# VectorE's low parts and the differential norm, moved from ahead of the next row maximum to behind it

## The chip, the core and the metric

The kernel runs on one core of one Trainium2 chip. The metric is the time of one execution on the device in microseconds (us); lower is better. The kernel before took 1900.06 us (median of three runs, 1899.64 to 1900.58).

## What is computed

A trunk of two layers on x of 512 x 1024 (float32). Each layer is a feed-forward block, a mixer and a second feed-forward block, each followed by a layer norm. The change touches the mixer alone:

```python
proj = x @ w_in
# FoX heads: 6 of width 64
s = einsum(q, k) * scale + (c_q - c_k);  p = softmax(causal(s));  y = p @ v
# differential heads: 4, each with two maps of width 32
p = softmax(causal(einsum(q, k) * scale - slope * dist))
a = p[0] - lam * p[1];  o = a @ v
o = o * rsqrt(mean(o * o) + eps) * norm_g * (1 - lam_init)
# SGU heads: 6
y_sgu = u * (tril(w_s) @ layer_norm(g) + b_s)
out = concatenate([y_fox, y_diff, y_sgu]) @ w_out
```

## The kernel before

Every large product is made of three matmuls: each float32 operand is split into a high part (ScalarE rounds it into an fp32r tile) and a low part (VectorE or GpSimd subtracts the high part from the original), and TensorE adds high x high, high x low and low x high. A low part is thus a subtraction that has to wait for ScalarE's copy. The whole program is written out by hand as one instruction list for each engine, with semaphores between them. No scheduler reorders anything: each engine takes its list in order, and a wait in it holds all that stands behind.

**The attention stage.** Per layer there are 5 bodies b = 0 to 4. A body is a pair of heads. Bodies 0, 2 and 4 are FoX, bodies 1 and 3 (`DIFF_AT`) are differential. A body has 8 steps k = 0 to 7: two heads times four blocks of 128 queries. The text numbers the 40 steps of a layer G = 8b + k. The block t = G mod 4 has (t+1)*128 keys, so steps get longer from t = 0 to t = 3.

In step G TensorE (`heads`, from L1276) issues, in this order: the scores of step G (L1291, and the mask L1293), three matmuls of other work, the value products of step G-2 (L1313), the transposes of the probabilities of step G-1 (L1303), three more matmuls of other work. The other work is a generator: in bodies 0 to 2 the projection of the queries and keys of body b+2 (`project`, L1216; queries in the body's steps k = 0 to 3, keys in k = 4 to 7), in bodies 3 and 4 the output projection with the head chunks that are ready (`early_output`, L1011). In four steps, (b,k) = (0,1), (0,5), (2,1) and (2,5), so G = 1, 5, 17 and 21, four transposes of a chunk of the output (`turn_y`, L1242) close the step. They write into bank 7 or bank 6, the same PSUM banks that the projections use, and so wait for `qk_ok`, the count of query and key low parts done:

```python
pe.wait_ge(qk_ok, (l * BODIES + at[0] + 1) * 2 + (3 if at[1] > NT else 2))   # L1228
```

For G = 1 and G = 17 that is the key low part of body 1 and of body 3, for G = 5 and G = 21 the query low part of body 2 and of body 4: each is the part that VectorE does in that step's neighbourhood.

ScalarE in step G: `exp` of step G (L919, one for each map; it waits for the row maximum), `p_out` of step G-1 (L926, the copy of the transposed probabilities that the value products read), then at k = 0 the high part of the keys of body b+1 (L858) and half of a weight tile (`key_half`, L713), at k = 4 the high part of the queries of body b+2 (L851) and `query_half` (L713 too) of the weights of body b+3, and in the step after a `turn_y` its high part (`y_hi`, L932).

VectorE in step G: `row_max` (L1898, one for each map), `inverse` (L1905, a reciprocal, FoX only), `output` of step G-2 (L1930, which waits for that step's value products), `early_add` (L1540, bodies 3 and 4), in differential bodies `mix` (L1913, L1915, L1919: reciprocals, weight, and the sum of the two maps, which waits for both exponentials), and then the pieces that the change moves:

- `key(b+1)` at k = 0 (L1811): low part of the keys
- `query(b+2)` at k = 4 (L1806): low part of the queries
- `y_lo` (L1859): low part of an output chunk, in the step after its transposes, and in body 4 at k = 1, 2 and 7
- `rms` (L1874, L1878, L1885, L1890): the four stages of the differential norm, in bodies 2 and 4. GpSimd makes the reciprocal root between the second and the third (`norm_root`, L597 and L599)

SyncE (`put_query`, `put_key`, L462) then writes the query and key parts of a body to DRAM in 12 transfers each, and behind `put_key(b)` it loads the weights of body b+2 into the tile `rawA` (`fill`, L395), which `query_half` on ScalarE waits for. GpSimd loads the stacked queries and keys of a body back from DRAM (`load_stack`, L652) before its scores.

Of the kernel before, what the change touches and what calls it, by code (L numbers as in the profile page):

```python
# [48 lines left out]
BODIES = FOX_P + DIFF_P  # L49
# [12 lines left out]
STEPS = 2 * NT  # L62
# [13 lines left out]
ALL = BODIES * STEPS  # L76
# [45 lines left out]
def build(nc, x_in, a_w, b_w, d_w, gb_row, gb_col, mix_row, mix_col, ws_in, lamv, out):  # L122
    ctx = ExitStack()
    with ctx:
# [244 lines left out]
        def is_diff(G):  # L369
            return G // STEPS in DIFF_AT  # L370
# [1093 lines left out]
        def _(dve):  # L1464
# [329 lines left out]
            for l in range(L):  # L1794
# [98 lines left out]
                def row_max(G):  # L1893
                    w_ = (G % NT + 1) * P
                    for m in range(2 if is_diff(G) else 1):
                        i = 2 * (G % 2) + m
                        dve.wait_ge(s_done[m], count(l, G, m))
                        v.tensor_reduce(negm[:, i:i + 1], bank[i][:, 0:w_], AX.X, ALU.max,  # L1898
                                        negate=True).then_inc(max_ok[m], 1)
# [32 lines left out]
                query(1)  # L1932
                dve.wait_ge(nlam1_ok, l + 1)
                wait_here(5)
                for G in range(ALL):
                    b, k = divmod(G, STEPS)
                    row_max(G)
                    last_key = k == 0 and b == EARLY_BODY
                    if last_key:
                        key(b + 1)  # L1940
                    if G and not is_diff(G - 1):
                        inverse(G - 1)
                    if G >= 2:
                        output(G - 2)
                    if G - EARLY_BODY * STEPS in ADD_STEP:
                        early_add(ADD_STEP[G - EARLY_BODY * STEPS])
                    if is_diff(G):
                        mix(G)
                    if k == 0 and b + 1 < BODIES and not last_key:
                        key(b + 1)  # L1950
                    if k == NT and b < EARLY_BODY:
                        query(b + 2)
                    if (b, k - 1) in TURNS:
                        y_lo(TURN_AT.index((b, k - 1)))
                    if b == BODIES - 1 and k in LATE_TURNS:
                        y_lo(LATE_TURNS[k])
                    if b in RMS_AT and k in RMS_AT[b]:
                        rms(DIFF_AT.index(b - 1), RMS_AT[b].index(k))
                inverse(ALL - 1)
                output(ALL - 2)  # L1960
                early_add(6)
                early_add(7)
                output(ALL - 1)
# [91 lines left out]
```

## Time and profile before

| | |
|---|---|
| median of the runs | 1900.06 us (1899.64 to 1900.58) |
| the profiled execution, its own time | 1899.35 us |
| its span (first to last instruction) | 1897.6 us |
| busy: TensorE / VectorE / ScalarE / GpSimd | 98% / 74% / 39% / 11% |
| attention stage of layer 0 / layer 1 | about 461 to 572 us / 1398 to 1509 us of the span |
| mean granted TensorE clock | 0.998 |

The span is taken from one profiled execution; its own time is 1.75 us longer than its span and 0.7 us under the median. "PE" is TensorE's matmul unit and "PEld" its weight load, which runs a little ahead of the matmul that needs it; DVE is VectorE, ACT ScalarE, POOL GpSimd, SPq SyncE's queue. A wait is written behind a row in brackets: the idle time of the engine ahead of the instruction, and what ended it.

### The profile page before, as it was taken

The numbers are of one execution on the slowest core, as the hardware profiler recorded it, in microseconds if no ns is written. First come the engines' busy times: TensorE is split into PE (matmuls) and PEld (weight loads), VectorE is DVE, ScalarE is ACT, GpSimd is POOL, SyncE is SP. The second block draws the span as 40 slices with busy tenths as digits, with TensorE's granted clock in tenths as the row PEclk, the third lists the DMA queues.
The fourth block names the chain that finished last, engine by engine and source line by source line (L and its number), as shares of the span: only waits on it lengthen the run. The fifth ranks groups of instructions, "written<-read, shape, count | busy, mean of one in ns | idle before, by whom it ended". The sixth has DMA issues, their size and how long they took to land.

```text
span 1897.6 us, 25000 instructions
## 1 busy us (share of the span) xinstructions
PE 1867.6 (98%) x9121; PEld 1572.7 (83%) x9121; DVE 1411.4 (74%) x2059; ACT 741.0 (39%) x1114; POOL 217.0 (11%) x247
## 2 busy tenths in 40 slices
PE   7999999999999999999999999999999999999998
PEld 6888888889888888888888888888888888888886
DVE  7877877952676878787897777777536688777777
ACT  5332333434554423333253242423455543424243
POOL 2000000153323000000100000003343220000001
PEclk9999999999999999999999999999999999999999
DMA  5222223236742222222313222223557323222221
GB/s 215 100 111 88 111 88 133 91 119 179 207 115 90 111 88 111 88 111 88 133 69 131 89 111 88 111 111 107 153 156 210 89 83 115 111 88 111 88 111 45
DMA packets 43747, 215.95 MB, mean 114 GB/s; under 512 B 8756, under 2 KB 11252, under 8 KB 20008
## 3 DMA queue, kind: packets, MB, share of 16 engines
q1 hardware_dynamic: 40808, 199.30, 29.7%
q0 software_dynamic: 2880, 15.90, 3.6%
q8 instruction: 33, 0.54, 0.1%
q14 instruction: 26, 0.21, 0.0%
HBM read 197.23 MB, written 17.93 MB: 113 GB/s over the span
## 4 chain that ended last, share of the span: by engine, by line
PE 90%; DVE 5%; issue 2%; ACT 1%; DMA 1%; POOL 1%; SPq 0%; ACTq 0%; DVEq 0%; POOLq 0%
PE psum L1011 80%; PE psum L1216 5%; PE psum L1313 2%; DVE res L1540 1%; PE psum L1303 1%; PE psum L1042 1%; PE psum L1291 1%; DVE st L1557 1%; DVE negm L1898 1%; DVE xlo L1496 0%; DMA gbc<-in_gb_col 0%; PE psum L1415 0%; PE psum L1242 0%; POOL rstd L609 0%; ACT psum L919 0%
## 5 line engine op out<-in xcount | busy, mean ns | idle before, releaser
L1011 PE MATMUL psum<-xhi,whiA 128*128 128x512 f32 (+1 forms) x768 | 287.4, 374 | 4.9 <-DVE xlo L1496 4.9
L1011 PE MATMUL psum<-xlo,whiA 128*128 128x512 f32 (+1 forms) x768 | 285.9, 372 | 0.0
L1011 PE MATMUL psum<-xhi,wloA 128*128 128x512 f32 (+1 forms) x768 | 285.8, 372 | 0.0
L1011 PE MATMUL psum<-xhi,whiB 128*128 128x512 f32 x704 | 273.9, 389 | 0.0
L1011 PE MATMUL psum<-xlo,whiB 128*128 128x512 f32 x704 | 273.9, 389 | 0.0
L1011 PE MATMUL psum<-xhi,wloB 128*128 128x512 f32 x704 | 273.9, 389 | 0.0
L1011 PE MATMUL psum<-whiD,hl 128*128 128x512 f32 x768 | 264.0, 390 | 2.0 <-DVE wloD L1473 2.0
L799 ACT ACTIVATE s<-psum 128x512 f32<-128x512 f32 x40 | 23.9, 598 | 540.7 <-PE psum L1011 540.6
L1651 DVE SCALAR_TENSOR_TENSOR res<-psum,res 128x1024 f32<-128x1024 f32 x120 | 146.7, 1222 | 82.1 <-PE psum L1011 82.1
L1651 DVE SCALAR_TENSOR_TENSOR nat<-psum,nat 128x1024 f32<-128x1024 f32 x144 | 175.8, 1221 | 26.3 <-PE psum L1011 26.3
L1011 PEld LDWEIGHTS psum<-xhi,whiA 128*128 128x128 f32 x768 | 145.4, 189 | 32.4 <-DVE xlo L1496 6.0
L1011 PEld LDWEIGHTS psum<-whiD,hl 128*128 128x128 f32 x768 | 144.2, 188 | 32.6 <-issue 2.4
L1011 PE MATMUL psum<-thi,hl 128*128 128x512 f32 x480 | 167.2, 389 | 0.0
L1011 PEld LDWEIGHTS psum<-xlo,whiA 128*128 128x128 f32 x768 | 145.4, 189 | 25.2
L1011 PEld LDWEIGHTS psum<-xhi,wloA 128*128 128x128 f32 x768 | 145.4, 189 | 24.9
L1473 DVE TENSOR_TENSOR wloA<-rawA,whiA 128x2048 fp32r<-128x2048 f32 x50 | 118.8, 2375 | 57.0 <-ACT whiA L706 57.0
L1011 PEld LDWEIGHTS psum<-xlo,whiB 128*128 128x128 f32 x704 | 132.1, 188 | 27.4
L1011 PEld LDWEIGHTS psum<-xhi,wloB 128*128 128x128 f32 x704 | 132.1, 188 | 27.4
L1011 PEld LDWEIGHTS psum<-xhi,whiB 128*128 128x128 f32 x704 | 132.1, 188 | 27.3
L1011 PE MATMUL psum<-wloD,hl 128*128 128x512 f32 x384 | 149.4, 389 | 0.0
L1473 DVE TENSOR_TENSOR wloB<-rawB,whiB 128x2048 fp32r<-128x2048 f32 x49 | 111.9, 2284 | 18.5 <-ACT whiB L706 18.5
L569 POOL TENSOR_TENSOR gbr<-gbr,alpha 128x1024 f32<-128x1024 f32 x6 | 11.2, 1896 | 937.1 <-DMA gbr<-in_gb_row 937.1
(230 smaller groups left out, 3520.5 us busy)
## 6 DMA issues: line engine op xcount, KB each, us to landing
rawA<-in_a_w SPq DMA_DIRECT2D x62, 1024.0 KB, 6.3
rawB<-in_b_w SPq DMA_DIRECT2D x54, 1024.0 KB, 4.8
rawD<-in_d_w SPq DMA_DIRECT2D x46, 1024.0 KB, 4.7
stacks<-hl SPq DMA_DIRECT2D x192, 64.0 KB, 1.7
whiD<-stacks POOLq DMA_DIRECT2D x10, 768.0 KB, 6.4
wloD<-stacks POOLq DMA_DIRECT2D x10, 768.0 KB, 5.9
gbr<-in_gb_row SPq DMA_DIRECT2D x6, 1024.0 KB, 8.4
stacks<-wloD SPq DMA_DIRECT2D x48, 64.0 KB, 1.7
```

The lines of the kernel that those rows point to most:

```text
L799: a.activation(silu["A"], bank[0][:, :], ACT.Silu).then_inc(silu_ok["A"], 1)
L1011: ins = t_.matmul(out_, a_, b_, start=(start and k == 1), stop=(stop and k == n), skip_group_check=check)
L1042: ins = t_.transpose(bank[b][:, lo:lo + P], src[:, 2 * h + t, c * P:c * P + P], ident[:, :])
L1216: ins = t_.matmul(bank[6 + g][:, :], a_, b_, start=(k == 1), stop=(k == 3 * NC))
L1291: t_.matmul(bank[i][:, 0:n_], tile[0:STACK, n, t * P:t * P + P], tile[0:STACK, 2 + n, 0:n_], start=(n == 0 or maps == 2), stop=False)
L1303: ins = t_.transpose(bank[4 + G % 2][:, e * P:e * P + P], s32[:, 2 * (G % 2), e * P:e * P + P], ident[:, :])
L1313: ins = t_.matmul(bank[4 + G % 2][:, 0:HD], pt[G % 2][:, e * P:e * P + P], vals[:, e, vc:vc + HD], start=(e == 0), stop=(e == t))
L1473: v.tensor_tensor(wlo[s][:, :], raw[s][:, :], f32(whi[s][:, :]), ALU.subtract).then_inc(lo_ok[s], 1)
L1540: v.scalar_tensor_tensor(out=r, in0=bank[b][:, :], scalar=scale, in1=r, op0=ALU.mult, op1=ALU.add).then_inc(step, 1)
L1557: v.bn_stats(st[:, t, hf, :], res[:, t, hf * 512:hf * 512 + 512]).then_inc(st_ok, 1)
L1651: v.scalar_tensor_tensor(out=to, in0=psum[:, 4 + k % 2 * 2:6 + k % 2 * 2, :], scalar=0.5 * sign, in1=to, op0=ALU.mult, op1=ALU.add).then_i ...
L1898: v.tensor_reduce(negm[:, i:i + 1], bank[i][:, 0:w_], AX.X, ALU.max, negate=True).then_inc(max_ok[m], 1)
```

## The change

The six conditional pieces at the end of a step (all but the key part at G = 24, which stays where it is) become a function `aside(G)`. It is called one step later: in step G the loop now does `row_max(G)`, `inverse(G-1)`, `output(G-2)`, the early addition, then `aside(G-1)`, then `mix(G)`. No instruction is added or removed, and no other engine's list is touched.

```diff
-                for G in range(ALL):
+                def aside(G):
                     b, k = divmod(G, STEPS)
-                    row_max(G)
-                    last_key = k == 0 and b == EARLY_BODY
-                    if last_key:
-                        key(b + 1)
-                    if G and not is_diff(G - 1):
-                        inverse(G - 1)
-                    if G >= 2:
-                        output(G - 2)
-                    if G - EARLY_BODY * STEPS in ADD_STEP:
-                        early_add(ADD_STEP[G - EARLY_BODY * STEPS])
-                    if is_diff(G):
-                        mix(G)
-                    if k == 0 and b + 1 < BODIES and not last_key:
+                    if k == 0 and b + 1 < BODIES and b != EARLY_BODY:
                         key(b + 1)
                     if k == NT and b < EARLY_BODY:
                         query(b + 2)
...
                     if b in RMS_AT and k in RMS_AT[b]:
                         rms(DIFF_AT.index(b - 1), RMS_AT[b].index(k))
+
+                for G in range(ALL):
+                    b, k = divmod(G, STEPS)
+                    row_max(G)
+                    if k == 0 and b == EARLY_BODY:
+                        key(b + 1)
+                    if G and not is_diff(G - 1):
+                        inverse(G - 1)
+                    if G >= 2:
+                        output(G - 2)
+                    if G - EARLY_BODY * STEPS in ADD_STEP:
+                        early_add(ADD_STEP[G - EARLY_BODY * STEPS])
+                    if G:
+                        aside(G - 1)
+                    if is_diff(G):
+                        mix(G)
                 inverse(ALL - 1)
                 output(ALL - 2)
+                aside(ALL - 1)
```

**How VectorE's list moves, body 0.** Around steps 4 and 5 of body 0 it reads, before (the query part of step 4, then step 5's row maximum, reciprocal and output, then step 6's row maximum):

```order
L1806 SCALAR_TENSOR_TENSOR hl<-psum,qscale,hl 128x512
L1898 TENSOR_REDUCE negm<-psum 128x1
L1905 RECIPROCAL rinv<-rsum 128x1
L1930 TENSOR_SCALAR nat<-psum,rinv 128x64
L1898 TENSOR_REDUCE negm<-psum 128x1
```

and with the change, from step 5's row maximum on:

```order
L1898 TENSOR_REDUCE negm<-psum 128x1
L1905 RECIPROCAL rinv<-rsum 128x1
L1930 TENSOR_SCALAR nat<-psum,rinv 128x64
L1806 SCALAR_TENSOR_TENSOR hl<-psum,qscale,hl 128x512
L1898 TENSOR_REDUCE negm<-psum 128x1
```

The query part (L1806) has moved behind three instructions of step 5, the last of which (L1930) waits for TensorE's value products of step 3.

**Body 1.** The same for the key part, around steps 8 and 9. Before (step 8's mix, the key part, then step 9):

```order
L1919 SCALAR_TENSOR_TENSOR s<-psum,wlam,s 128x128
L1811 TENSOR_TENSOR hl<-psum,hl 128x512
L1898 TENSOR_REDUCE negm<-psum 128x1 x2
L1930 TENSOR_SCALAR nat<-psum,rinv 128x64
L1913 RECIPROCAL rinv<-rsum 128x2
L1915 TENSOR_SCALAR wlam<-rinv,rsum,nlam 128x1
L1919 SCALAR_TENSOR_TENSOR s<-psum,wlam,s 128x256
```

and now:

```order
L1919 SCALAR_TENSOR_TENSOR s<-psum,wlam,s 128x128
L1898 TENSOR_REDUCE negm<-psum 128x1 x2
L1930 TENSOR_SCALAR nat<-psum,rinv 128x64
L1811 TENSOR_TENSOR hl<-psum,hl 128x512
L1913 RECIPROCAL rinv<-rsum 128x2
L1915 TENSOR_SCALAR wlam<-rinv,rsum,nlam 128x1
L1919 SCALAR_TENSOR_TENSOR s<-psum,wlam,s 128x256
```

The key part (L1811) has moved behind both row maxima and the output (L1930), and stands directly ahead of step 9's mix (L1913 to L1919).

**Body 4.** Steps 33 to 35 on VectorE, from the low part of step 33 on. Before:

```order
L1859 TENSOR_TENSOR xlo<-psum,xhi 128x512
L1898 TENSOR_REDUCE negm<-psum 128x1
L1905 RECIPROCAL rinv<-rsum 128x1
L1930 TENSOR_SCALAR nat<-psum,rinv 128x64
L1540 SCALAR_TENSOR_TENSOR res<-psum,res 128x512
L1859 TENSOR_TENSOR xlo<-psum,xhi 128x512
L1874 SCALAR_TENSOR_TENSOR mix<-nat 128x512
L1898 TENSOR_REDUCE negm<-psum 128x1
```

and now, from step 34's row maximum on:

```order
L1898 TENSOR_REDUCE negm<-psum 128x1
L1905 RECIPROCAL rinv<-rsum 128x1
L1930 TENSOR_SCALAR nat<-psum,rinv 128x64
L1540 SCALAR_TENSOR_TENSOR res<-psum,res 128x512
L1859 TENSOR_TENSOR xlo<-psum,xhi 128x512
L1898 TENSOR_REDUCE negm<-psum 128x1
L1905 RECIPROCAL rinv<-rsum 128x1
L1930 TENSOR_SCALAR nat<-psum,rinv 128x64
L1859 TENSOR_TENSOR xlo<-psum,xhi 128x512
L1874 SCALAR_TENSOR_TENSOR mix<-nat 128x512
```

Step 35's row maximum (the second L1898) no longer has the second low part and the norm's first stage (L1859, L1874) ahead of it.

## Rows read from the trace of the kernel before

**Rows 1.** The page's chain that ended last, by engine

```profile
PE 90%; DVE 5%; issue 2%; ACT 1%; DMA 1%; POOL 1%; SPq 0%; ACTq 0%; DVEq 0%; POOLq 0%
```

**Rows 2.** Waits of the weight loads, 461 to 581 us: total, times, longest

```profile
PEld psum L1313 <- ACT s L926: 2.4, 4, 1.2
```

**Rows 3.** Timeline, layer 0, step 5: start us, duration us, engine, line, instruction

```profile
474.20 0.75 DVE L1806 SCALAR_TENSOR_TENSOR hl<-psum,qscale,hl 128x512 fp32r<-128x512 f32 x1 [1.37 <-ACT hl L851]
475.58 0.28 DVE L1930 TENSOR_SCALAR nat<-psum,rinv 128x64 f32<-128x64 f32 x1 [0.23 <-PE psum L1313]
475.98 0.59 PEld L1242 LDWEIGHTS psum<-ident,nat 128*128 128x128 f32 x4
```

**Rows 4.** Timeline, layer 0, step 17

```profile
508.36 0.69 DVE L1811 TENSOR_TENSOR hl<-psum,hl 128x512 fp32r<-128x512 f32 x1 [1.48 <-ACT hl L858]
509.82 0.28 DVE L1930 TENSOR_SCALAR nat<-psum,rinv 128x64 f32<-128x64 f32 x1 [0.36 <-PE psum L1313]
510.20 0.59 PEld L1242 LDWEIGHTS psum<-ident,nat 128*128 128x128 f32 x4
```

**Rows 5.** Timeline, layer 0, step 1

```profile
463.51 0.69 DVE L1811 TENSOR_TENSOR hl<-psum,hl 128x512 fp32r<-128x512 f32 x1 [1.01 <-ACT hl L858]
465.07 0.59 PEld L1242 LDWEIGHTS psum<-ident,nat 128*128 128x128 f32 x4
```

**Rows 6.** Timeline, layer 0, steps 8 and 9

```profile
484.98 1.06 ACT L713 ACTIVATE whiA<-rawA 128x1024 fp32r<-128x1024 f32 x1
485.13 0.69 DVE L1811 TENSOR_TENSOR hl<-psum,hl 128x512 fp32r<-128x512 f32 x1 [0.51 <-ACT hl L858]
486.70 0.28 DVE L1930 TENSOR_SCALAR nat<-psum,rinv 128x64 f32<-128x64 f32 x1 [0.21 <-PE psum L1313]
487.31 0.17 DVE L1913 RECIPROCAL rinv<-rsum 128x2 f32<-128x2 f32 x1 [0.33 <-ACT psum L919]
```

**Rows 7.** The chain that ended last, layer 0, end of body 1

```profile
505.74 0.76 DVE s L1919
```

**Rows 8.** Layer 0, body 1: puts, landing of the weights behind them, step 13's exponential

```profile
485.85 5.46 SPq L462 DMA_DIRECT2D stacks<-hl  x12
DMA to landing us min/median/max: 4.9/4.9/4.9
497.96 0.48 ACT L919 ACTIVATE s<-psum,negm 128x256 f32<-128x256 f32 x1 [0.21 <-DVE negm L1898]
```

**Rows 9.** Timeline, layer 1, step 12: the half copy

```profile
1433.83 1.06 ACT L713 ACTIVATE whiA<-rawA 128x1024 fp32r<-128x1024 f32 x1 [0.37 <-DMA rawA<-in_a_w]
```

**Rows 10.** Timeline: half copies and value products, layer 1 body 0 and layer 0 body 2

```profile
1412.60 1.06 ACT L713 ACTIVATE whiA<-rawA 128x1024 fp32r<-128x1024 f32 x1 [1.90 <-DMA rawA<-in_a_w]
1414.34 0.30 PEld L1313 LDWEIGHTS psum<-vals,s 128*128 128x128 f32 x2 [0.26 <-ACT s L926]
520.80 1.06 ACT L713 ACTIVATE whiA<-rawA 128x1024 fp32r<-128x1024 f32 x1 [1.52 <-DMA rawA<-in_a_w]
522.67 0.42 PEld L1313 LDWEIGHTS psum<-vals,s 128*128 128x128 f32 x2
```

**Rows 11.** Timeline, layer 0, steps 34 to 36 of body 4

```profile
556.36 0.19 PEld L1293 LDWEIGHTS psum<-maskr,identr 128*128 128x128 f32 x1
558.83 0.68 DVE L1898 TENSOR_REDUCE negm<-psum 128x1 f32<-128x512 f32 x1
560.76 0.30 PEld L1313 LDWEIGHTS psum<-vals,s 128*128 128x128 f32 x2 [1.19 <-ACT s L926]
```

**Rows 12.** Timeline, layer 0, start of body 3

```profile
527.75 0.41 PEld L1313 LDWEIGHTS psum<-vals,s 128*128 128x128 f32 x3 [0.19 <-ACT s L926]
```

**Rows 13.** Stack load of body 3 on GpSimd, its landing, and the scores that need it

```profile
518.27 1.09 POOL L652 DMA_DIRECT2D whiD<-stacks  x2
DMA to landing us min/median/max: 2.9/4.4/5.9
526.46 0.19 PEld L1291 LDWEIGHTS psum<-whiD 97*128 97x128 f32 x1
```

## The prediction

> **What bounds the kernel now.** I read the chain that ended last first: TensorE carries 90% of it [rows 1]. So a piece of VectorE's work costs or saves time only where TensorE waits for it, or where the chain itself leaves TensorE. Then the waits of TensorE's weight loads in the attention stage, the only stage that the change touches: in layer 0 they waited four times for the copy of the transposed probabilities, 2.4 us in all, and 1.2 us of that is one wait [rows 2]. Layer 1 repeats this with one more wait. That is the first thing to see: all that a faster row maximum could win is a few microseconds of 1900. The second is how near other waits are. I took the timeline of every step in which a piece moves and looked for who needs that piece next: the transposes of an output chunk, SyncE's puts with the weight load behind them, and the next mix.
>
> The profiled execution took 1899.35 us, 0.7 us under the median; the sum below is a difference, and I add it to the median of 1900.06.
>
> **What the move does to a piece.** A piece leaves the end of step G and goes behind the row maximum, the reciprocal and the output of step G+1. The first two are cheap. The output (L1930) is not: it waits for value products that TensorE issues after the scores of step G+1. So the piece is now tied to TensorE's own progress inside that step, and TensorE comes to the next thing that needs it soon after.
>
> **Transposes that wait for the piece (cost).** Step 5: before, the query part ran at 474.20 for 0.75 us. The output of step 3 started at 475.58, and TensorE came to the transposes at 475.98 [rows 3]. With the change the query part starts when the output lets go of VectorE. In steps 8 and 9 the next start after a 0.28 us instruction can be 0.2 us later, which I take: 475.78. It ends at 476.53, and the transposes load at about 476.57, 0.6 us late. Since a load runs ahead of its matmul, I count 0.5. Step 17: the output is at 509.82, so the key part (0.69 us [rows 6]) ends at 510.71, where the transposes came at 510.20 [rows 4]: 0.5. Step 21 has step 5's order (query part behind the output): 0.5. Step 1 has no output ahead of it, since outputs begin in step 2. The key part ended at 464.20 and the transposes came at 465.07 [rows 5]; it moves by one reduction and one reciprocal, about a microsecond later with the wait for the scores: 0.1. Together 1.6 per layer, **3.2 for both**. Bounds: nothing, if TensorE had room here; but no wait and no gap stands before these loads in rows 3 and 4, so the lost time has no cover, and I keep close to the upper end of 0.6 each.
>
> **The loop of body 1 (cost).** In body 1 the chain leaves TensorE: mix, row maxima, two exponentials and the next mix follow each other until the last mix at 505.74 [rows 7]. Two pieces sat in this loop, the key part (0.61 us to the next start) and the query part (0.67). It looks as if they were won. They are not. At step 9 the exponential cannot start before ScalarE has finished its half copy, at 486.04 [rows 6], so it stays about where it was. And the key part, behind the output at 486.70, now ends its share at 487.5, where the mix of step 9 began at 487.31 [rows 6]: 0.2 lost instead. Step 12 is alike for the query part: the half copy ends at 497.75, and the exponential started at 497.96 [rows 8], so 0.2 won at best.
>
> What decides is SyncE. The key part ended at 485.82, the 12 puts began at 485.85 and ended at 491.31, and the weights right behind them landed 4.9 after their issue, at 496.2 [rows 6, 8]. Now the key part ends at 486.70 + 0.2 + 0.69 = 487.59, 1.77 later, and so do the puts, the load and the landing: 498.0. The half copy in front of step 13's exponential needs the weights and takes 1.06 [rows 6], so the exponential starts at about 499.06 instead of 497.96 [rows 8], **1.1 late in layer 0**. In layer 1 the half copy already waited for this transfer, by 0.37 us [rows 9], so all of the delay counts: **1.75**. The 0.2 of step 9 is inside these. Nothing hides them, because the loop is the chain [rows 7]. Bounds: nothing (if the puts or the load speed up), and 1.8 in each layer.
>
> The Trainium skill, in "DMA: Bandwidth & Descriptors", section "Anatomy of one DMA — SWDGE (gpsimd) path", fits a transfer as 2.0 us and the bytes by 436 GB/s; for 1 MB that is an estimate of 4.4 us. The trace does not agree: 4.9 in rows 8, beside other transfers. If the moved load ran at the page's price, both terms would be 0.5 smaller and the sum 3.4 instead of 4.4.
>
> **The same wait in other bodies (cost).** In layer 1, body 0, the half copy waited until 1412.60, and the value products behind it started 1.74 later, at 1414.34, after waiting [rows 10]. Key part, puts and load move by about 0.95 (one reduction, one reciprocal and the wait for the scores), TensorE itself by the 0.5 of step 5: **0.4**. In layer 0, body 2, the copy started at 520.80 [rows 10]. Its key part ended at 509.05 [rows 4], so its load is 510.71 - 509.05 = 1.66 later, so the value products can start at 520.80 + 1.66 + 1.74 = 524.2; TensorE, itself 1.0 late, comes at 522.67 + 1.0: **0.45**.
>
> **What is won.** Step 35's scores were loaded at 556.36, but its row maximum started only at 558.83, behind the early addition, an output low part and the norm's first stage; the value products then waited 1.19 [rows 11]. Now only the addition and step 33's low part stand ahead: the row maximum starts at about 557.1, 1.7 earlier, more than the wait. I take 1.1 per layer, since something small may come next (step 38's copy was ready within 0.1 of its need). At the start of body 3 a wait of 0.19 goes the same way [rows 12]: 0.15. **-2.5 for both layers.** Bounds: 0 to -2.8.
>
> All other pieces (the low parts of steps 2, 6 and 39, the norm's later stages) I cost at nothing. Their cover is TensorE's work until it needs the chunk, a whole step or more. The norm's second stage has a thin one, taken up below.
>
> **Sum:** 3.2 + 1.1 + 1.75 + 0.4 + 0.45 - 2.5 = +4.4 us, so **1904.5 us**. About 0.2% (3.8 us) is what a measurement of this kernel can tell from no change; the forecast lies just beyond it, on the slower side.
>
> **Rivals.**
>
> *The weights come in time.* If the transfer waits in bodies 0, 1 and 2 do not grow, say because the puts meet less other traffic, 3.7 goes out of the sum: +0.7, 1900.8. For it: the load of rows 9 was waited for by only 0.37, so a little speed would do much. Against: the puts followed the key part within 0.03 us. With half of that kept, 1902.6: no change that can be measured. Chance 0.33 with all that lies between.
>
> *The row maximum leads (faster).* The place is the loop of bodies 1 and 3 and step 35. If the outputs were ready when VectorE reached them, the moved pieces would run while ScalarE does its exponentials: 0.61 + 0.67 per layer in body 1, 1.19 + 0.19 behind, together 2.66 per layer, 1894.7. It decides where the output's value products end before the row maxima do. In rows 3, 4 and 6 they end after, with VectorE idle before the output each time, so I give it 0.07.
>
> *The stack load of body 3 comes late (slower still).* The norm's second stage moves behind the output of step 18, and GpSimd's root and stack load, at 518.27, stand behind it. They move by 2.3; the slower of the two loads landed 5.9 after its issue, so at about 524.7, and now at 527.0, while the scores come at 526.46 [rows 13] and 0.9 later by the terms above. Half a microsecond of room in layer 0, none in layer 1. Should it run over, or step 35's gain go to the next wait, 2 to 3 more: 1907. Chance 0.18.
>
> The forecast itself (1903 to 1906) has 0.42; about a third of that lies within 3.8 us of no change. So faster 0.07, within 0.2% 0.42, slower 0.51. The range, 1899.8 to 1907.8, takes in the case with the weights in time and most of the late stack load, and leaves out the faster case.
>
> **What would show it.** Right: the transposes (L1242) of steps 5, 17 and 21 wait for VectorE's L1806 or L1811 about 0.5 us; the half copy at step 12 waits 1 to 2 us for rawA in both layers; the wait of 1.19 before L1313 in body 4 is gone. Wrong, if L1242 has no wait before it; if the puts of body 1 start less than 1.5 us later against the mix of step 8; or if a new wait of over a microsecond stands in body 3 or 4.

## The result, and the profile after

| | before | with the change |
|---|---|---|
| median of the runs, us | 1900.16 (8 runs, one of them far off) | 1906.81 (8 runs, 1902.39 to 1910.82) |
| the profiled execution, own time, us | 1899.35 | 1906.7 |
| its span, us | 1897.6 | 1905.0 |

One of the eight runs of the kernel before took 3119.34 us, for a reason that nothing here shows; the other seven took 1899.20 to 1900.59. The ratio is 1.0038, 95% interval 1.0028 to 1.0049: the change makes the kernel slower, by 6.65 us between the medians and by 7.2 us by the ratio. I had predicted 4.4 us more, 1904.5, with a range up to 1907.8. The direction was the likeliest case, the size is half as large again.

The page's chain that ended last, of the changed kernel, by engine:

```profile
PE 89%; DVE 5%; DMA 2%; issue 2%; SPq 1%; ACT 1%; POOL 1%; ACTq 0%; DVEq 0%; POOLq 0%
```

Against [rows 1], TensorE gives a point to DMA and to SyncE's queue, which stood at 1% and 0%. That points to a transfer and to the puts in front of it. The waits of TensorE's weight loads in layer 0, 461 to 581 us (engine, line, what it waited for: total us, times, longest):

```profile
PEld psum L1313 <- ACT s L926: 4.9, 5, 2.2
PEld psum L1303 <- DVE s L1919: 1.5, 5, 0.6
PEld psum L1242 <- DVE hl L1806: 1.3, 2, 0.6
PEld psum L1242 <- DVE hl L1811: 0.6, 1, 0.6
PEld psum L1291 <- DMA whiD<-stacks: 0.2, 1, 0.2
```

Read it against [rows 2], where L1313 stood at 2.4 us in 4 waits and L1242 was absent. The transposes now wait three times, 0.6 us each. The waits of L1313 have grown to 4.9 us in 5, though the one of 1.2 in body 4 is gone from them: a new one of 2.2 has come in body 0 and one of 1.1 in body 2.

**Where the time went.** I cut the attention stage at the first score load of each body and, at the end, of step 39. Durations in us, worked out from the start times in the timeline of the weight loads:

| | body 0 | body 1 | body 2 | body 3 | body 4, to step 39 | sum |
|---|---|---|---|---|---|---|
| layer 0 before | 19.88 | 22.57 | 22.51 | 21.94 | 18.37 | 105.27 |
| layer 0 change | 22.32 | 24.06 | 24.15 | 21.93 | 17.36 | 109.82 |
| layer 1 before | 19.96 | 22.76 | 22.55 | 22.19 | 18.39 | 105.85 |
| layer 1 change | 21.00 | 23.99 | 23.87 | 22.18 | 17.37 | 108.41 |

The stages differ by 4.55 + 2.56 = 7.1 us, of 7.4 between the spans. The granted TensorE clock was 1.00 (2.4 GHz) all through these stages in both profiled executions, so no part of the 7.1 us is the clock's. Body 4 wins 1.0 in each layer, and bodies 0 to 2 lose 5.6 and 3.6.

**Body 0 of layer 0** is the worst. VectorE, ScalarE and the weight loads there, from three answers of the timeline (start us, duration us, engine, line, operation, out<-in, and in brackets the idle time before and its releaser):

```profile
476.09 0.28 DVE L1930 TENSOR_SCALAR nat<-psum,rinv 128x64 f32<-128x64 f32 x1 [1.10 <-PE psum L1313]
476.29 0.74 DVE L1806 SCALAR_TENSOR_TENSOR hl<-psum,qscale,hl 128x512 fp32r<-128x512 f32 x1
```

```profile
477.09 0.42 PEld L1242 LDWEIGHTS psum<-ident,nat 128*128 128x128 f32 x4 [0.64 <-DVE hl L1806]
...
480.66 0.30 PEld L1313 LDWEIGHTS psum<-vals,s 128*128 128x128 f32 x2 [2.17 <-ACT s L926]
```

```profile
478.93 1.06 ACT L713 ACTIVATE whiA<-rawA 128x1024 fp32r<-128x1024 f32 x1 [4.26 <-DMA rawA<-in_a_w]
```

Follow it backwards. The query part starts 0.20 after the output and TensorE's transposes wait for it, as the prediction's step 5 had it. Then the value products wait 2.17 us for a copy of the probabilities, which ScalarE makes behind its half copy of weights (L713), and that waits 4.26 us for a transfer. SyncE's queue and the landing of this transfer, in the DMA view of 471 to 474 us (out<-in, queue, count, KB each, us to landing):

```profile
rawA<-in_a_w SPq DMA_DIRECT2D x1, 1024.0 KB, 7.6
whiD<-stacks POOLq DMA_DIRECT2D x1, 768.0 KB, 7.2
```

It was issued at 471.22 instead of 469.79, and it took 7.6 us instead of 5.5. The body itself began 0.50 later, so the issue was 0.93 late within it. The later issue I had foreseen (0.95), the slower landing not.

**Body 1** has the load of step 12, which the prediction rested on. SyncE, then ScalarE:

```profile
490.57 5.47 SPq L462 DMA_DIRECT2D stacks<-hl  x12
...
496.08 0.43 SPq L395 DMA_DIRECT2D rawA<-in_a_w  x1
```

```profile
501.27 1.06 ACT L713 ACTIVATE whiA<-rawA 128x1024 fp32r<-128x1024 f32 x1 [1.31 <-DMA rawA<-in_a_w]
```

The puts start when the key part (L1811, now at 489.86 behind the output of 489.66) ends, and take 5.5 us as in [rows 8]. Against the mix of step 8 (484.27 before, 487.21 now) they start 1.78 later. The half copy, which had not waited in layer 0, waits 1.31 us, and 1.43 in layer 1.

**A thing I had not looked for**, in body 2 of layer 1. VectorE, then GpSimd:

```profile
1466.13 3.08 DVE L1885 TENSOR_TENSOR nat<-nat,drs 128x128 f32<-128x128 f32 x4
1469.13 0.55 DVE L1898 TENSOR_REDUCE negm<-psum 128x1 f32<-128x384 f32 x1
```

```profile
1466.43 2.42 POOL L633 TENSOR_TENSOR wloA<-rawA,whiA 128x1024 fp32r<-128x1024 f32 x1 [0.24 <-ACT whiA L713]
```

and the view of the line L1885 there (count, and shortest, median and longest in ns):

```profile
L1885 DVE TENSOR_TENSOR nat<-nat,drs x4: 279/281/2472, 1466.1 to 1468.9; 128x128 f32<-128x128 f32 x4
```

Four small multiplications of the norm take 3.08 us together. The same four are 0.89 us in layer 0, where no such instruction of GpSimd runs beside them. The third took 2.47 us, and it ends at 1469.00, 0.15 after GpSimd's low half of weights. The row maximum behind them starts at 1469.13, and TensorE waits 0.68 us.

### The profile page after: what moved, and what is told of

It reads as the page before. It is cut to its first block, busy times and chain, and to the rows that moved or that the text cites. A ratio compares the mean times of both kernels' runs of the same rounds, so it can differ in the third digit from the quotient of the medians.

```text
span 1905.0 us, 25000 instructions
## 1 busy us (share of the span) xinstructions
PE 1869.6 (98%) x9121; PEld 1571.1 (82%) x9121; DVE 1413.5 (74%) x2059; ACT 741.4 (39%) x1114; POOL 216.2 (11%) x247
## 4 chain that ended last, share of the span: by engine, by line
PE 89%; DVE 5%; DMA 2%; issue 2%; SPq 1%; ACT 1%; POOL 1%; ACTq 0%; DVEq 0%; POOLq 0%
PE psum L1011 80%; PE psum L1216 4%; PE psum L1313 1%; DMA rawA<-in_a_w 1%; SPq L462 1%; DVE res L1540 1%; PE psum L1042 1%; DVE st L1557 1%; PE psum L1303 1%; PE psum L1291 1%; DVE xlo L1496 0%; DMA gbc<-in_gb_col 0%; DVE negm L1898 0%; PE psum L1415 0%; DVE xhi L1492 0%
```

## The experiments

The theory: the change costs where a piece that others need at once was tied to the output, that is keys and queries; the norm and the output's low parts win in body 4. Its parts were first tried apart. "before" is always that of the same batch: 1899.24 us in the first, 1899.4 in the second, 1899.34 in the third. In the diffs `aside` is what the change does one step later, and `here` is called at the end of a step.

### norm_late: only the low parts of output chunks and the norm move

```diff
                 def aside(G):
...
-                    if k == 0 and b + 1 < BODIES and b != EARLY_BODY:
-                        key(b + 1)
-                    if k == NT and b < EARLY_BODY:
-                        query(b + 2)
...
+                def here(G):
+                    b, k = divmod(G, STEPS)
+                    if k == 0 and b + 1 < BODIES and b != EARLY_BODY:
+                        key(b + 1)
+                    if k == NT and b < EARLY_BODY:
+                        query(b + 2)
```

> Only the output low parts and the norm stages move one step later; key and query low parts stay where they were. Theory A (the key and query parts, tied to the output's value products, cost; the row maximum of step 35 gains): no wait before the transposes L1242, no longer wait for rawA than before, the 1.19 us wait before L1313 in body 4 gone in both layers: 2.2 us faster than before, about 1897.9. Rival B (the late norm costs, by a late stack load of body 3 or by VectorE and GpSimd in each other's way): no faster than before, 1901 or more, with a wait of L1291 for the stacks or a long L1885.

Measured: 1899.81 us (11 runs), ratio 1.0005 [0.9996, 1.0014]. No cost that can be told, but no gain either: theory A's 1897.9 is missed, and the time lies under the 1901 of rival B, whose signs are all there. The waits of the weight loads, 461 to 581 us:

```profile
PEld psum L1313 <- ACT s L926: 1.5, 3, 0.6
PEld psum L1291 <- DMA whiD<-stacks: 1.2, 1, 1.2
PEld psum L1303 <- DVE s L1919: 0.7, 3, 0.2
```

Body 4 lasts 17.37 and 17.36: the gain is there. It is lost in body 2, which takes 23.96 and 23.66 instead of 22.5. In layer 0 a score load waits 1.18 us for the stacks: GpSimd's root starts at 518.56 and its stack load is issued at 520.47, 2.2 us later than in [rows 13]. This is the rival of the late stack load. In layer 1 it is the long L1885:

```profile
1459.06 3.89 DVE L1885 TENSOR_TENSOR nat<-nat,drs 128x128 f32<-128x128 f32 x4
1462.88 0.54 DVE L1898 TENSOR_REDUCE negm<-psum 128x1 f32<-128x384 f32 x1
```

with L633 on GpSimd from 1459.79 to 1462.19, and 1.27 us of waiting before L1313. Body 0 of layer 1 also took 21.24 instead of 19.96, behind a weight load that landed after 6.4 us, although its key part had not moved.

### keys_late: only keys and queries move

```diff
                 def aside(G):
...
-                    if (b, k - 1) in TURNS:
-                        y_lo(TURN_AT.index((b, k - 1)))
-                    if b == BODIES - 1 and k in LATE_TURNS:
-                        y_lo(LATE_TURNS[k])
-                    if b in RMS_AT and k in RMS_AT[b]:
-                        rms(DIFF_AT.index(b - 1), RMS_AT[b].index(k))
...
+                def here(G):
...
```

(`here` has the six lines.)

> Only the key and query low parts move one step later. Theory A: all costs of the change and none of its gain: 6.7 + 2.2 = 8.9 us slower than before, about 1909, with waits of 0.6 us before L1242 at steps 5, 17 and 21 in each layer, long waits of the half copy L713 for rawA, and the 1.19 us wait in body 4 still there. Rival B (the norm costs): within 2 us of before.

Measured: 1906.35 us (5 runs), ratio 1.0039 [1.0026, 1.0052]: 7.1 us slower, where 8.9 was expected, and as much as the whole change costs. The waits of L1242 are those of the change, 0.64, 0.60 and 0.66 in each layer, and body 4 keeps its old 18.4. Rival B (within 2 us of before) falls.

### before_output: every piece behind the row maximum, but ahead of the output

```diff
                     row_max(G)
                     if k == 0 and b == EARLY_BODY:
                         key(b + 1)
+                    if G:
+                        aside(G - 1)
                     if G and not is_diff(G - 1):
                         inverse(G - 1)
                     if G >= 2:
                         output(G - 2)
...
-                    if G:
-                        aside(G - 1)
```

> All pieces move behind the next row maximum, but ahead of the reciprocal and the output. Theory A (the output's wait for value products is what makes the move dear): query part of step 4 ends at about 475.1, before the transposes at 475.98; no L1242 waits; body 1's key part 0.6 us later instead of 1.8; the gain in body 4 stays: 0.7 - 2.2 = 1.5 us faster than before, about 1898.6. Rival C (any place behind the row maximum is too late): within 2 us of the change, 1905 to 1909.

Measured: 1900.59 us (12 runs, 1897.25 to 1905.73), ratio 1.0008 [0.9999, 1.0016]. The waits of 461 to 581 us:

```profile
PEld psum L1313 <- ACT s L926: 3.5, 3, 2.7
PEld psum L1303 <- DVE s L1919: 0.9, 4, 0.2
```

No transposes wait (L1242 is absent), bodies 1 and 2 of layer 0 last 22.43 and 22.55 as before, and body 4 17.37. Rival C falls. By the two ratios (1.0038 and 1.0008), 5.7 us of what the change costs go with the place behind the output. The place ahead of it is not free either: the time was to be 1898.6 and is 1.35 us over the kernel before, although body 4 gives 2.0 back. In this profile most of that stands in body 0 of layer 0, which lasts 23.96 instead of 19.88. The weights again took 7.7 us to land, and L1313 waits 2.68. Behind that wait comes a second loss. The view of the busy time by stretches (stretch; its length; busy time and count of PE, PEld, DVE, ACT and POOL; granted clock, DMA share, GB/s):

```profile
476.00:478.00 2.00, 0.65 (x3) 0.19 (x1) 0.50 (x1) 0.83 (x1) 0.00 (x0) 1.00 0.83 238
480.00:482.00 2.00, 2.00 (x8) 1.62 (x7) 0.99 (x2) 0.73 (x2) 1.15 (x2) 0.61 0.39 99
482.00:484.00 2.00, 2.00 (x10) 1.86 (x10) 0.65 (x3) 0.73 (x3) 0.54 (x2) 0.54 0.43 82
```

The granted clock fell from 2.4 to 1.2 GHz at 480.4, for 3.4 us, with TensorE busy all the time; half of 3.4 is 1.7 us, an estimate of what it cost. With the 2.24 us that TensorE's matmuls stood idle, that makes 3.9 of the 4.1. In key_late (below) a wait of 2.71 left the clock at 1.00, so a wait of this length does not always bring it down. Body 2 of layer 1 lasts 23.17 instead of 22.55, with a wait of 0.68 for the stacks.

### weights_first: the change, with the weight load issued ahead of the key's puts

```diff
                     put_query(b)
-                    put_key(b)
                     fill("A", l * A_ALL + A_QK + b + 2)
+                    put_key(b)
```

> The change as it is, and SyncE loads the next weights (fill A) ahead of the 12 key puts instead of behind them. Theory A (the weights come late because the load stands behind the puts, which start with the key part): the waits of L713 for rawA fall under 0.5 us, the 0.6 us waits before L1242 stay: 4 to 5 us faster than the change, about 1902. Rival D (the load is slow because of other transfers, wherever it is issued): L713 still waits over 1 us in three bodies or more and the time stays within 1.5 us of 1906.8; or the puts, now behind the load, make the stack loads late, seen as waits of L1291 for DMA.

Measured: 1905.41 us (5 runs), ratio 1.0033 [1.0021, 1.0046], 1.4 us under the change where theory A had 4 to 5. No half copy waits for weights any more, so its reason for the late weights holds, and its time does not. The waits of 461 to 581 us:

```profile
PEld psum L1291 <- DMA whiD<-stacks: 2.5, 2, 2.0
PEld psum L1313 <- ACT s L926: 1.8, 3, 1.0
PEld psum L1242 <- DVE hl L1806: 1.3, 2, 0.6
PEld psum L1303 <- DVE s L1919: 0.7, 3, 0.2
PEld psum L1242 <- DVE hl L1811: 0.6, 1, 0.6
```

Now the stacks are late in layer 0, by 2.0 and 0.5 us, as rival D's last case had it: whichever of puts and weights goes second in SyncE's queue is waited for once the key part is late. L1885 is long in both layers, 3.42 and 3.23 us. And behind the wait of 2.0 the clock fell here too, from 483.5 on for 3.4 us:

```profile
484.00:486.00 2.00, 2.00 (x12) 1.98 (x10) 0.53 (x3) 0.15 (x2) 0.00 (x0) 0.50 0.91 208
```

By the same estimate that is 1.7 us in this profile, in body 1 of layer 0, which lasts 24.59.

### body4_late: only body 4's low parts and norm stages move

```diff
                 def aside(G):

                     b, k = divmod(G, STEPS)
+                    if b == BODIES - 1 and k in LATE_TURNS:
+                        y_lo(LATE_TURNS[k])
+                    if b == BODIES - 1 and k in RMS_AT[b]:
+                        rms(DIFF_AT.index(b - 1), RMS_AT[b].index(k))
```

(the rest of `aside` has gone to `here`.)

> Only body 4's output low parts and norm stages go behind the next step's row maximum; all else runs where it ran before. Theory A (the gain of the change is body 4's alone, and norm_late lost it again in body 2): the wait of 1.19 us before L1313 is gone in both layers, body 4 up to step 39 takes 17.4 us instead of 18.4, bodies 0 to 3 are as before, so 2.0 us less: ratio 0.9989 against the kernel before, about 1897.2 where that one takes 1899.2. Rival B (a microsecond won at step 35 is given back behind the stage, since the last outputs and the output projection wait for something else): body 4 is shorter but the span is not, ratio within 0.0003 of 1.

Measured: 1896.72 us (11 runs, 1895.77 to 1897.99), ratio 0.9988 [0.9979, 0.9997]. The waits of 461 to 581 us:

```profile
PEld psum L1313 <- ACT s L926: 1.2, 3, 0.6
PEld psum L1303 <- DVE s L1919: 0.7, 3, 0.2
```

Body 4 takes 17.38 and 17.37, bodies 0 to 3 stand within 0.11 us of before, and rival B, that the microsecond is given back behind the stage, falls. This is the version that beats both kernels: 2.7 us under the one before by the medians (the interval allows 0.6 to 4.0), and by the two ratios about 9.5 under the change. In the two profiles the ten bodies together are 2.2 us shorter.

### lows_late: as body4_late, and the low parts of turned chunks too

```diff
                 def aside(G):

                     b, k = divmod(G, STEPS)
+                    if (b, k - 1) in TURNS:
+                        y_lo(TURN_AT.index((b, k - 1)))
                     if b == BODIES - 1 and k in LATE_TURNS:
                         y_lo(LATE_TURNS[k])
```

> As body4_late, and the low parts of the turned output chunks in bodies 0, 2 and 3 also go behind the next row maximum; body 2's norm stages, the keys and the queries stay. Theory A (it was body 2's norm stages that made norm_late lose in body 2): bodies 2 last 22.5 us as before, no load L1291 waits for the stacks, no L1885 takes over 1.5 us, and the time is within 0.4 us of body4_late, ratio 0.9988. Rival B (the low parts behind the row maximum cost it): bodies 2 last 23.7 to 24.0 as in norm_late, ratio 1.0000 to 1.0010.

Measured: 1897.68 us (11 runs), ratio 0.9990 [0.9981, 0.9999], a microsecond above body4_late in the medians; the intervals overlap. No load L1291 waits for the stacks, and bodies 2 last 22.76 and 22.58, not the 24.0 and 23.7 of norm_late: it was body 2's norm stages that lost there. Theory A's time (within 0.4 us of body4_late) was missed by the medians. No L1885 was long, but a row of four L1890, also of the norm, took 1.88 us under an L633 in layer 0. That layer's body 1 also lasted 23.18 here, behind a weight load that took 6.2 us to land instead of 4.9 in body4_late.

### key_late and query_late: the two halves of keys_late

```diff
                 def aside(G):

                     b, k = divmod(G, STEPS)
                     if k == 0 and b + 1 < BODIES and b != EARLY_BODY:
                         key(b + 1)
-                    if k == NT and b < EARLY_BODY:
-                        query(b + 2)
...
```

(This is key_late. In query_late `aside` keeps the query's two lines alone, and all else goes to `here`.)

> Only the low parts of the keys go behind the next step's output. Theory A (keys cost by the puts and the weight load behind them, queries only by the transposes): L1242 waits once per layer for it, at step 17, 0.6 us; the half copies L713 wait for rawA 1.3 to 4 us in bodies 0 to 2 as in keys_late; the 7.1 us of keys_late less four waits of 0.6, so 4.7 us slower than before, ratio 1.0025. Rival B (the queries' part in the loop of body 1 and in front of body 2's copy is what delays the scores): the key alone costs under 2.5 us, ratio under 1.0013.

Measured: 1907.72 us (5 runs), ratio 1.0040 [1.0026, 1.0053], 8.3 us slower. L1242 waits 0.6 us at step 17, as theory A has it, but 4.7 us was expected for all: a miss in size. Rival B (under 2.5) falls.

> Only the low parts of the queries go behind the next step's output. Theory A: L1242 waits 0.6 us at steps 5 and 21 in each layer and nothing else changes, since the puts of a query come long after it: 2.4 us slower than before, ratio 1.0013. Rival B (those waits only take time from waits that come later): ratio 1.0000 to 1.0004. Rival C (the queries cost as much as the keys): 4 us or more, ratio 1.0021.

Measured: 1901.1 us (11 runs), ratio 1.0009 [1.0000, 1.0018], 1.7 us. The transposes wait four times, 0.64 or 0.65 us each, in bodies 0 and 2 of both layers, and these four bodies last 0.36 to 0.48 us longer than before, 1.7 in sum. So a wait of 0.64 costs 0.43 us here; I had counted 0.5. Together the two cost more than keys_late (10.0 against 7.1), so they don't add up. In key_late L1313 waits 2.71 and 2.01 us in bodies 0 and 2 of layer 0, behind half copies that wait 4.36 and 3.66 for rawA; so much of the key's cost is in how late weights land, and that varies from profile to profile. Theory A of query_late is right in its four waits, and its price of 2.4 us is 0.7 too high.

### key0_in_place: the change, with body 0's key part in its old place

```diff
                 def aside(G):
...
-                    if k == 0 and b + 1 < BODIES and b != EARLY_BODY:
+                    if k == 0 and 0 < b and b + 1 < BODIES and b != EARLY_BODY:
                         key(b + 1)
...
                     if is_diff(G):
                         mix(G)
+                    if G == 0:
+                        key(1)
```

> The change, with the key part of step 0 (the one whose puts are followed by the weight load of body 0) back at the end of its own step. In the profiled runs so far the weight load of body 0 in layer 0 lands 7.1 to 7.7 us after its issue wherever this key part is moved and 5.4 to 5.6 wherever it is not. Theory A (the moved key part makes the load late and slow): the landing is 5.4 to 5.7 us, the half copy of body 0 waits under 1.6 us, the wait of 2.17 us before L1313 is gone and body 0 of layer 0 lasts 20.3 us instead of 22.3, of layer 1 20.3 instead of 21.0: 2.7 us less than the change, about 1904 where that one takes 1906.8, ratio 1.0023. Rival B (the slow landing comes with something else that the runs had in common): body 0 of layer 0 still lasts over 21.5 us.

Measured: 1903.42 us (11 runs), ratio 1.0021 [1.0012, 1.0030], 3.4 us under the change. The weights of body 0 landed after (DMA view of 467 to 474 us)

```profile
rawA<-in_a_w SPq DMA_DIRECT2D x1, 1024.0 KB, 5.3
```

and body 0 lasts 20.32 us in both layers, as expected to a few hundredths. Six profiled kernels with this key part in place show 5.3 to 5.6 us in layer 0, and the four with it moved, ahead of or behind the output, 7.1 to 7.7 (not counting the three that also change the order or the time of the transfers). So in layer 0 the slow landing goes with the moved key part. In layer 1 it does not: moved, it took 5.2 in keys_late and before_output, 5.5 in key_late and 6.4 in the change; in place, 4.9 to 5.6 and once 6.4 (norm_late). Each is one profiled execution.

### stack_waits: the change, with GpSimd's stack load held until the weights have landed

```diff
                 for b in range(EARLY_BODY):
                     if b - 1 in DIFF_AT:
                         norm_root(DIFF_AT.index(b - 1))
+                    if b == 0:
+                        pool.wait_ge(landed["A"], 16 * (l * A_ALL + A_QK + 4))
                     load_stack(b + 1, 0)
```

> The change, and GpSimd issues the stack load of body 1 only once the weights of body 0's load have landed, so that the two transfers no longer run beside each other. Theory A (the 768 KB stack load beside it is what stretches the 1 MB weight load): the weights land 4.0 to 5.2 us after their issue in both layers and L1313 has no wait in body 0; the stack load moves by 3 to 4 us, lands about 483 in layer 0, and may be waited for by the first scores of body 1, by up to 2 us. Rival B (the load is slow by itself or by the puts): the landing stays over 6.3 us in both layers.

Measured: 1904.23 us (6 runs), ratio 1.0028 [1.0016, 1.0040]. The DMA view of 467 to 474 us, and the waits of 461 to 581 (lines from 676 on are two higher in this kernel, so L1293 is the change's L1291):

```profile
rawA<-in_a_w SPq DMA_DIRECT2D x1, 1024.0 KB, 5.2
```

```profile
PEld psum L1315 <- ACT s L928: 2.1, 4, 0.6
PEld psum L1293 <- DMA whiD<-stacks: 1.8, 2, 1.5
```

With no stack load beside it the transfer takes 5.2 us in layer 0 and 4.9 in layer 1, with the key part moved as in the change (7.6 and 6.4), and the waits of 2.17 and 0.87 in body 0 are gone. So the slow landing needs the stack load beside it, but that is not enough: in the kernel before, the same two transfers were issued 1.75 us apart as well, and the weights landed in 5.5. In place of the old waits the first scores of body 1 wait 1.47 and 1.51 us for the stacks, as theory A allowed. Body 0 lasts 21.73 and 21.77, and all bodies together are only 1.1 us shorter than the change's.

The packet records of the traces show where the 2 us go. The weights travel in packets of 8 KB, and the first packet of the stack load starts 3.9 to 4.3 us after the weights' issue (6.4 and 6.7 here, where it is held back). This load is there twice, once per layer, in each of the eleven profiles that keep the order of SyncE's list. In the 16 cases that landed within 5.6 us the last 8 KB packet started at most 4.6 us after the issue; in the six that took 6.4 to 7.7, two to four stragglers started later than that, the last at 5.0 to 6.5, among the packets of the stack load. So a slow landing is a few late packets and not a slow transfer. What leaves them over, in layer 0 just when the key part has moved, stays open.

### quarters: weights_first, with GpSimd's low halves in two pieces each

```diff
-                    c = slice(h * D, h * D + D)
-                    g.tensor_tensor(wlo[s][:, c], raw[s][:, c], whi[s][:, c].bitcast(F32), ALU.subtract).then_inc(lo_done, 1)
+                    m = (h * D + D // 2)
+                    g.tensor_tensor(wlo[s][:, h * D:m], raw[s][:, h * D:m], whi[s][:, h * D:m].bitcast(F32), ALU.subtract)
+                    g.tensor_tensor(wlo[s][:, m:h * D + D], raw[s][:, m:h * D + D], whi[s][:, m:h * D + D].bitcast(F32), ALU.subtract).then_inc(lo_done, 1)
```

> As weights_first, with each of GpSimd's low parts L633 (one tensor_tensor of 128x1024, 2.4 us) issued as two of 128x512; the result is the same. In weights_first the row of four L1885 took 3.42 us in layer 0 and 3.23 in layer 1, where they met an L633. Theory A (a VectorE operation with two SBUF inputs is held until GpSimd's instruction ends): no L1885 row lasts over 2.3 us, L1313's waits of 1.02 and 0.82 shrink to under 0.3, some 1.2 us less than weights_first. Rival B (the two share bandwidth and the piece size does not matter): the L1885 rows last 3 us or more again.

Measured: 1904.43 us (8 runs), ratio 1.0029 [1.0019, 1.0040]. VectorE, then GpSimd, in layer 0 (L1887 is the norm's multiplication, L634 and L635 the two pieces):

```profile
525.12 3.68 DVE L1887 TENSOR_TENSOR nat<-nat,drs 128x128 f32<-128x128 f32 x4
528.72 0.55 DVE L1900 TENSOR_REDUCE negm<-psum 128x1 f32<-128x384 f32 x1
```

```profile
525.68 1.32 POOL L634 TENSOR_TENSOR wloA<-rawA,whiA 128x512 fp32r<-128x512 f32 x1
526.93 1.30 POOL L635 TENSOR_TENSOR wloA<-rawA,whiA 128x512 fp32r<-128x512 f32 x1
```

Theory A, "until GpSimd's instruction ends", falls in this form, and so does its forecast for L1315 (waits of 1.28 and 0.96, not under 0.3). The longest L1887 took 3.08 us, which is more than one piece of 1.3: VectorE was held from 525.3 to 528.4, through both. It got nothing in the seam between two pieces that follow each other without a gap. Rival B named the right length (the rows of four last 3.68 and 3.36 us), but shared bandwidth does not fit the ends: in all seven such cases of the five profiles that have one, the long instruction ended 0.15 or 0.16 us after GpSimd's, whether it had begun 1.26 us behind it or 0.73 ahead of it. The time is 1.0 us under weights_first by the medians, within the two intervals, and the rows give no reason for it; the clock fell in this profile too, for 3.4 us from 483.6 on, behind a wait of 2.42 for the stacks.

## Why the prediction was right, and where its sizes were off

By its own steps, with the sum of the bodies as the measure (layer 0 / layer 1, us against before):

| | predicted | measured |
|---|---|---|
| body 0 | +0.6 / +1.0 | +2.44 / +1.04 |
| body 1 | +1.1 / +1.75 | +1.49 / +1.23 |
| body 2 | +1.45 / +1.0 | +1.64 / +1.32 |
| body 3 | -0.15 / -0.15 | -0.01 / -0.01 |
| body 4 | -1.1 / -1.1 | -1.01 / -1.02 |

- **"Transposes that wait for the piece (cost)"** was right in place, number and size. Steps 5, 17 and 21 wait 0.64, 0.60 and 0.64 us in both layers, for L1806, L1811, L1806; step 1 does not wait. query_late puts the price of one at 0.43 us, and before_output, where they vanish, shows that the output was the reason. That is 0.07 under the 0.5 that I had counted for each.
- **"The loop of body 1 (cost)"** was right in its chain: key part, 12 puts, load, half copy. Its sum for two layers, 2.85, measured 2.7. The puts moved by 1.78 where I had 1.77. The split was off, in part since the landing in layer 1 took 4.8 us instead of 5.1; that the sum came out so near is in part luck. The fit of the Trainium skill that I set beside this term is, by its section's title, one for transfers that GpSimd issues, and this load is SyncE's, so the comparison says little.
- **"The same wait in other bodies (cost)"** is the step that failed in size. (Its term for body 2 of layer 0 was also added up wrong: 524.2 against 523.67 is 0.53, not 0.45, and the sum 4.5.) It took the landing of the weights from before, and asked only how much later they were issued. For body 0 of layer 0 it found nothing to pay; the landing went from 5.5 to 7.6 us and 1.84 us were lost. stack_waits shows that it takes GpSimd's stack load beside it to be this slow, and key0_in_place that in layer 0 it goes with the moved key part. How the one leads to the other is not shown. These 1.84 us are two thirds of what was missing in the sum (7.1 - 4.4 = 2.7); the smaller misses partly cancel, body 1 of layer 1 by 0.52 against body 1 of layer 0 and body 2.
- **"All other pieces ... I cost at nothing"** missed two things. The late stack load of body 3, which I kept as a rival, costs 1.2 us in norm_late and hardly shows in the change, where TensorE is late itself. The other I had not thought of: the norm's multiplications land under GpSimd's low half of weights.
- **"What is won"** was right for body 4 (1.0 per layer, I took 1.1) and wrong for body 3. The wait of 0.19 is gone in both layers, yet the body is not shorter.
- **The rivals.** "The weights come in time" fell: the half copies waited 1.3 to 4.3 us. "The row maximum leads" fell as argued, since outputs come after the row maxima. That a piece behind the output inherits the output's wait was the right reason for the cost: keys_late and before_output show it, and body4_late separates the gain from it.

## What to carry to other kernels

Before a piece of work is moved later on one engine, look for the next instruction on that engine that waits for someone else: behind it the piece inherits that wait, and all who need the piece inherit it too. A list that wins in one place and loses in another should be cut by place; here one body of five held all of the gain, and moving that one alone gave 2.7 us where moving all five cost 6.7. A wait of TensorE can cost more than its own length when the granted clock falls behind it: look at the clock in the stretch that follows. A transfer's landing time is not a constant to be shifted in time with its issue, when another large transfer starts within its flight: carry it as a range.

## What the runs showed of the hardware

- **VectorE held by GpSimd.** A 128x128 fp32 tensor_tensor of VectorE with both inputs in SBUF takes 0.28 us alone. Beside GpSimd's tensor_tensor of 128x1024 (2.4 us) it took 2.47 us (the change), 3.29 (norm_late), 2.81 and 2.62 (weights_first), and ended 0.15 or 0.16 after GpSimd's. Beside GpSimd's issue of a stack load alone, four of them took their usual 0.89. Instructions of VectorE that read PSUM, or one SBUF tensor, show nothing of it: in the kernel before, 19 reciprocals of 128x1 ran beside such GpSimd instructions at 0.15 us each, and four row maxima of 128x512 at 0.68 to 0.69. Cutting GpSimd's instruction in two did not help, since the halves followed each other at once. The Trainium skill has this in "SBUF — State Buffer", section "SBUF: two separate sides": the port pair that VectorE and GpSimd share is locked for a whole instruction by whichever comes first, and a VectorE operation with two SBUF inputs takes part. The traces agree that the wait lasts to the end of GpSimd's instruction. They do not bear out that the first comer has it: in norm_late VectorE's instruction is recorded from 1459.06, 0.73 us before GpSimd's, and should have been done in 0.28 (GpSimd was then issuing its stack load, and its recorded times are rough). That VectorE got nothing between two GpSimd instructions is what the traces add.
- **Landing times and scatter.** The same 1 MB load took 4.8 to 7.7 us in the attention stages; the slow ones had a few packets left among those of another transfer. The 8 runs of the change spread over 8.4 us, the 27 of before in the second batch over 4.2 and the 11 of body4_late over 2.2. A landing on the chain may bring its scatter into the time, but the clock is a rival that no run rules out: of the 8 runs of the change, the three longest (1907.87 to 1910.82) had a mean granted clock of 0.996 to 0.997, the other five 0.998 or 0.999.
- **The clock behind a wait.** The granted clock fell to half for 3.4 us inside the attention stage in three of the thirteen profiles (before_output, weights_first, quarters), each time within 2 us of the end of a wait of 2.0 to 2.7 us. In the change (2.17) and in key_late (2.71) it did not fall.
- **A queue that is full.** Twelve puts of 64 KB keep SyncE's queue for 5.5 us. The weight load behind them (or, in weights_first, the puts behind the load) was waited for as soon as the key part moved by 1.8 us within body 1.
